# A hybrid transformer block on one core: softmax scaling and value evictions on ScalarE, the mLSTM's norm vector on transposed columns, one value product deferred

## The reference, cut to what matters

```python
# mLSTM branch
hm = mlstm_chunkwise(...)                                    # [B, S, 4, 256]
hm = hm * lax.rsqrt(jnp.mean(hm * hm, axis=-1, keepdims=True) + EPS)
hm = hm.reshape(B, S, M_WIDTH) * m_norm[i]
hm = jax.nn.sigmoid(m_o) * hm * jax.nn.silu(m_z)
# each of the three attentions
probs = jax.nn.softmax(logits, axis=-1);  out = probs @ v
# both branches
h = h + jnp.concatenate([hm, ha], axis=-1) @ w_out[i]
```

## Time and profile before

| | us |
|---|---|
| median of 3 runs (lowest, highest) | 889.74 (888.91, 890.21) |
| the profiled execution | 890.28 |
| its span from the first to the last instruction | 888.5 |
| PE busy / DVE / ACT / POOL | 854.0 / 667.8 / 451.8 / 68.4 |
| mean granted TensorE clock | 0.997 |

### The profile page before, as it was taken

How to read it: one execution, slowest core, us unless ns; L and a number is a source line. 1 busy time by engine, 2 the same in 40 slices (tenths; PEclk the granted TensorE clock), 3 DMA queues, 4 the chain that set the end, 5 groups by cost and what they waited for, 6 DMA issues and landing times.

```text
span 888.5 us, 14462 instructions
## 1 busy us (share of the span) xinstructions
PE 854.0 (96%) x5744; PEld 750.2 (84%) x5744; DVE 667.8 (75%) x1089; ACT 451.8 (51%) x719; POOL 68.4 (8%) x63
## 2 busy tenths in 40 slices
PE   8999989999999999999999999899999899999996
PEld 8989978767876898699999999579987899999995
DVE  5698798868977997789767848796777876556557
ACT  5464555454556555275454445265663654444450
POOL 1100001000001120011100100110000111001011
PEclk9999999999999999999999999999999999999998
DMA  8856677556965870899866896278617776656601
GB/s 325 305 167 193 193 237 240 180 167 201 339 236 208 276 266 1 339 328 385 278 215 224 291 354 229 94 277 332 223 45 298 287 299 202 204 163 190 191 1 47
DMA packets 56915, 200.65 MB, mean 226 GB/s; under 512 B 6600, under 2 KB 7936, under 8 KB 56848
## 3 DMA queue, kind: packets, MB, share of 16 engines
q1 hardware_dynamic: 55808, 196.50, 63.5%
q0 software_dynamic: 1040, 3.24, 1.1%
HBM read 198.57 MB, written 1.08 MB: 225 GB/s over the span
## 4 chain that ended last, share of the span: by engine, by line
PE 81%; DVE 11%; ACT 4%; issue 2%; DMA 1%; POOL 0%; DVEq 0%; SPq 0%
PE ps L1166 26%; PE ps L1167 25%; PE ps L1168 25%; DVE R L1467 2%; DVE wsp L1404 1%; PE ps L1179 1%; ACT pb L2107 1%; DVE wk L1442 1%; DMA X<-in_x 1%; PE ps L1333 1%; PE ps L1372 1%; PE ps L1258 1%; DVE small L1845 0%; PE ps L1341 0%; PE ps L1348 0%
## 5 line engine op out<-in xcount | busy, mean ns | idle before, releaser
L1166 PE MATMUL ps<-XT,wsp 128*128 128x256 f32 x760 | 215.2, 283 | 5.9 <-DVE XT L1449 3.0
L1167 PE MATMUL ps<-XT,wsp 128*128 128x256 f32 x760 | 212.5, 280 | 0.0
L1168 PE MATMUL ps<-XT,wsp 128*128 128x256 f32 x760 | 212.1, 279 | 0.0
L1404 DVE TENSOR_TENSOR wsp<-ring,wsp 128x1024 fp32r<-128x1024 f32 x141 | 175.2, 1251 | 9.1 <-ACT wsp L1949 9.0
L1949 ACT CAST wsp<-ring 128x1024 fp32r<-128x1024 f32 x140 | 145.5, 1045 | 60.7 <-PE ps L1168 53.8
L1166 PEld LDWEIGHTS ps<-XT,wsp 128*128 128x128 f32 x760 | 142.7, 188 | 10.6 <-DVE wsp L1404 4.1
L1167 PEld LDWEIGHTS ps<-XT,wsp 128*128 128x128 f32 x760 | 142.7, 188 | 0.9
L1168 PEld LDWEIGHTS ps<-XT,wsp 128*128 128x128 f32 x760 | 142.3, 187 | 0.0
L1166 PE MATMUL ps<-wsp,ra 128*128 128x512 f32 x236 | 94.5, 400 | 4.0 <-issue 1.5
L1168 PE MATMUL ps<-wsp,ra 128*128 128x512 f32 x236 | 93.6, 397 | 0.0
L1167 PE MATMUL ps<-wsp,ra 128*128 128x512 f32 x236 | 93.1, 394 | 0.0
(11 more groups left out here) (272 smaller groups left out, 1516.3 us busy)
## 6 DMA issues: line engine op xcount, KB each, us to landing
arena<-in_mod_w SPq DMA_DIRECT2D x48, 512.0 KB, 6.0
ring<-in_mod_w SPq DMA_DIRECT2D x44, 512.0 KB, 4.7
ring<-in_ffn_a SPq DMA_DIRECT2D x28, 512.0 KB, 5.0
ring<-in_ffn_b SPq DMA_DIRECT2D x28, 512.0 KB, 5.7
arena<-in_ffn_o SPq DMA_DIRECT2D x22, 512.0 KB, 4.8
ring<-in_ffn_o SPq DMA_DIRECT2D x22, 512.0 KB, 4.9
arena<-in_ffn_a SPq DMA_DIRECT2D x16, 512.0 KB, 5.1
arena<-in_ffn_b SPq DMA_DIRECT2D x16, 512.0 KB, 4.9
```

The lines of the kernel that those rows point to most:

```text
L1166: pe.matmul(o, l[0], r[0], start=start, stop=False)
L1167: pe.matmul(o, l[0], r[1], start=False, stop=False)
L1168: return pe.matmul(o, l[1], r[0], start=False, stop=stop)
L1404: ve.tensor_tensor(w[:, 1024:1024 + n], raw[slot[0]][:, 0:n], w[:, 0:n].bitcast(f32), SUB).then_inc(*done("V", "lo", u, also=[("raw", *slo ...
```

## The change

- `ev_mv` and `ev_av` are all done by ScalarE.
- The value products of the mLSTM's last head stand in the second yield of h == 4 and not in the first.
- `m_norm` lies among the constant columns. The multiplication by it in `ev_mz` and the two row loads are gone; the transposed columns of tags hm0 and hm1 are split by `xt_s` with `m_norm` as its scale, where `xt_hl` had no scale. `xt_s` now writes at the offset `k0`.
- `norm`: VectorE keeps the reciprocal; the scaling of the row is a ScalarE activation (Copy with a scale per partition). The place in the list of steps is the same.

```diff
@@ order()
-        add("ev_mv", t, cb, b, either())
+        add("ev_mv", t, cb, b, "A")
...
-                if h and j == 0:
+                if h and j == (h == 4):
...
-    proj_a("u", 8, "w_av", 0, 1, lambda t, cb, b: add("ev_av", t, b, either()))
+    proj_a("u", 8, "w_av", 0, 1, lambda t, cb, b: add("ev_av", t, b, "A"))
...
-        if t == 0:
-            rows_mn[c] = load(("row", "m_norm", c * 512), 512)
         s = wk.get()
-        add("ev_mz", t, c, b, s, prior("wk", s), rows_mn[c])
+        add("ev_mz", t, c, b, s, prior("wk", s))
         wk.put(s[0])
-        if t == 1:
-            free_raw(rows_mn[c])
...
-            transposed("hm0", 4, None)
+            transposed("hm0", 4, "s")
...
-            transposed("hm1", 4, None)
+            transposed("hm1", 4, "s")
@@ column()
+            if tag[0:2] == "hm":
+                return K("m_norm", 4 * int(tag[2]) + k), None, None
@@ vector()
-                        ve.scalar_tensor_tensor(d[1][k + i], ps[b[0]][:, i * 256:(i + 1) * 256], scale,
-                                                d[0][k + i].bitcast(f32), MUL, SUB).then_inc(
+                        ve.scalar_tensor_tensor(d[1][k0 + k + i], ps[b[0]][:, i * 256:(i + 1) * 256], scale,
+                                                d[0][k0 + k + i].bitcast(f32), MUL, SUB).then_inc(
...
                     ve.reciprocal(smx[:, i:i + 1], smx[:, i:i + 1]).then_inc(*done("V", "norm", task, i, 0))
-                    for e in new("V", ("norm", task, i, 0)):
-                        ve.wait_ge(*e)
-                    ve.tensor_scalar(p, p, smx[:, i:i + 1], None, MUL).then_inc(*done("V", "norm", task, i, 1))
...
-                    for e in new("V", ("mz", t, c, 1), ("ld", *mn)):
-                        ve.wait_ge(*e)
-                    ve.tensor_tensor(g, g, raw[mn[0]][:, 0:512], MUL).then_inc(
-                        *done("V", "mz", t, c, 2, also=[("raw", *mn)] if t else []))
@@ scalar()
-                        ac.activation(d[0][k + i], ps[b[0]][:, i * 256:(i + 1) * 256], ACT.Copy, scale=scale).then_inc(
+                        ac.activation(d[0][k0 + k + i], ps[b[0]][:, i * 256:(i + 1) * 256], ACT.Copy, scale=scale).then_inc(
...
+                elif kind == "norm":
+                    task, i, s = a
+                    p = pb[s[0]][:, 0:128 * (of(task, i)[1] + 1)]
+                    for e in new("A", ("norm", task, i, 0)):
+                        ac.wait_ge(*e)
+                    ac.activation(p, p, ACT.Copy, scale=smx[:, i:i + 1]).then_inc(*done("A", "norm", task, i, 1))
@@ layout()
-    o["m_norm"], o["norm_final"] = a["m_norm"], a["norm_final"].reshape(1, -1)
+    put("m_norm", col(a["m_norm"].reshape(-1)))
+    o["norm_final"] = a["norm_final"].reshape(1, -1)
```

More of the change, by code:

```diff
@@ L7 @@
 COLS = [("norm_in", 8), ("conv_w", 32), ("fconv_w", 132), ("fconv_b", 44), ("q_norm", 2), ("kv_norm", 2),
-        ("mod_b", 96), ("c", 8), ("b_gate", 2), ("inv_freq", 1), ("sign", 1), ("nf", 8), ("ln", 64)]
+        ("mod_b", 96), ("c", 8), ("b_gate", 2), ("inv_freq", 1), ("sign", 1), ("nf", 8), ("ln", 64),
+        ("m_norm", 8)]
 CONSTS = [("ident", 128), ("ones", 256), ("cm", 256), ("cmT", 256)]
@@ L640, in order @@
     dsa = W.beside(dsa_steps(), DSA_PACE)
-    rows_mn = {}
     def ev_moz(t, cb, b):
@@ L1672, in vector @@
                     task, i, s = a
-                    p = pb[s[0]][:, 0:128 * (of(task, i)[1] + 1)]
                     for e in new("V", ("exp", task, i)):
@@ L1701, in vector @@
                 elif kind == "ev_mz":
-                    t, c, b, s, _, mn = a
+                    t, c, b, s, _ = a
                     g = GT[:, t, c * 512:(c + 1) * 512]
@@ L1720, in vector @@
                             o = hm[:, t * 4 + h, :]
-                            for e in new("V", ("ml_rs",), ("mz", t, c, 2)):
+                            for e in new("V", ("ml_rs",), ("mz", t, c, 1)):
                                 ve.wait_ge(*e)
@@ L2132, in scalar @@
                 elif kind == "ev_mz":
-                    t, c, b, s, before, _ = a
+                    t, c, b, s, before = a
                     for e in new("A", ("fill", *b), before):
```

## The result

| | before | after |
|---|---|---|
| median (lowest, highest), us | 889.74 (888.91, 890.21) | 898.29 (897.26, 898.70) |
| the profiled execution, us | 890.28 | 898.7 |
| its span, us | 888.5 | 896.9 |
| mean granted TensorE clock | 0.997 | 0.992 |

The ratio is 1.0092 with a 95% interval of 1.0081 to 1.0103: the change makes the kernel 8.55 us slower. Slower was the forecast, but by 3.6 us, and the time lies above the range given.

The account below looks back on a forecast made before the run. TensorE, busy 854.0 of 888.5 us, was taken as the bound. Terms -0.8 - 0.2 + 3.4 + 1.2 = +3.6 us took the profiled 890.28 to 893.9, as median 893.3 us; range 888.4 to 896.5.

Parts of the forecast that it names:

- Evictions and the deferred product: mLSTM, 119 to 131 us: TensorE's wait moves from the value product to the weights' low halves; 0 us.
- The norm vector: Waits near 184 us and the next group: fewer VectorE multiplies against a longer split; -0.8 and -0.2 us.
- The second attention: Burst, 326 to 350 us: multiplies lengthen ScalarE and VectorE's alternation; maximum 3.2 us later, TensorE +3.4 us.
- what decides is the order: Softmax rows: the multiply stands behind an unrelated exp, ahead of the transposed rows' copy and the output's high half.
- The third attention's tail: 655 to 667 us: two turns with multiplies delay an output by 0.7 and the last multiply by 1.4; +1.2 us.
- its ends: The lowest and highest cost given for the third attention's tail: 0 and +1.8 us.
- the first one: Whole kernel: with the clock at 0.997 throughout, only changes to TensorE's idle time count; no size given.
- rings: Second attention's burst and third's tail: ScalarE and VectorE take turns, each multiply lengthens a turn; +4.6 us together.
- gates: The two waits around the mLSTM's gates and split, reached earlier without the norm vector's multiplies; -1.0 us together.
- faster: Rival, chance 0.18: banks and row buffers let TensorE run ahead, VectorE's relief alone counts; -2.9, 886.9 us.
- no change: Rival, chance 0.20: TensorE's slack in projection units takes most; tail costs 0.6 + 0.5 against 1.0 gained; 889.8 us.
- Slower still: Rival inside the forecast's 0.62: the multiply occupies ScalarE for its full 0.50 and 0.39 us; 894.8 us.

Follow-up runs that it names:

- evictions_and_deferral: The kernel before with only the value evictions on ScalarE and the last head's value products one unit later: 889.62 us, ratio 0.9991.
- all_but_rows_aligned: The changed kernel with VectorE scaling the softmax's rows again and 12 more unused constant columns: 887.59 us, 0.9967 of the kernel before.
- rows_only: The kernel before with only the scaling of the softmax's rows moved to ScalarE: 895.85 us, ratio 1.0064.
- change_aligned: The changed kernel with 12 unused columns behind the norm vector in the constant table: 893.68 us, 1.0039 of the kernel before.
- rows_behind_copy: The kernel before with all rows scaled on ScalarE, the multiply moved behind the copy of the transposed rows: 895.73 us, ratio 1.0055.
- aligned_again: A second measurement of the changed kernel with VectorE scaling the rows and 12 more unused constant columns: 886.98 us, 0.9961 of the kernel before.
- aligned_and_fitted: The changed kernel with VectorE scaling rows, 12 more unused columns and 9 unread multiplications in the layer norm's wait: 887.52 us, 0.9969 of before.

## Why the prediction was off

- **Evictions and the deferred product, 0:** right. `evictions_and_deferral` is equal to before within its interval, and the path is as forecast: the six small instructions stand before the next low half, TensorE is at the same matmul at 128.8 us.
- **The norm vector, -0.8 and -0.2:** the mechanism was right, the first size too large for the whole change. From 175 to 185 us the changed kernel gains 0.47, `all_but_rows_aligned` 0.77: the 0.3 between them is the rows on ScalarE, which alone cost 0.29 in that stretch of `rows_only` (`change_aligned` gains 0.49 there, with the rows on ScalarE). The prediction counted one multiply ahead of the split and also took the relief of VectorE. From 185 to 215 us the gain is 0.2 to 0.3. Measured -0.68 for -1.0.
- **The second attention, +3.4:** right in size, +3.80 from 326 to 350 us, heads of 4.27 us where 4.2 or more was forecast. Of its reason ("what decides is the order") half holds: the multiply lengthens the turn because it stands in it, but not because it stands ahead of the copy, as `rows_behind_copy` shows. In `rows_only` the maximum of 347.75 comes 3.20 us later, which is the sum's 3.2. By single steps its last four turns are as forecast, +0.67, +0.51, +0.68 and +0.48; the two ahead of them are -0.39 and +1.50 for 1.23 forecast together, and that they come out near it is luck. TensorE's idle time from 334 to 354 us is 2.7 us, not above 3, and only 1.28 of it ends with the multiply; the other waits end with an output's low half (L1689). The multiply's price, 0.50 and 0.39 us, was near: 510 and 385 ns.

```profile
L2104 ACT ACTIVATE pb<-pb,small x48: 385/443/510, 145.3 to 671.9; 128x128 f32<-128x128 f32 x24, 128x256 f32<-128x256 f32 x24
```

- **The third attention's tail, +1.2:** right as to the waits, +1.48, +1.48 and +1.43 in the three kernels with all rows on ScalarE and no fall behind the tail, within its ends.
- **The failed step** is the first one: "the granted clock is 0.997 throughout: only what adds to or takes from TensorE's idle time counts". It read the clock of before as a property of the kernel, and priced idle time by its own length. In the profiled execution TensorE was idle for 2.75 of the 24 us of the burst, where it had been for 1.03, and across the burst's end for 1.28 us in one piece, up to 350.80; from 352.81 on it ran at 1.2 GHz for 3.4 us: +1.50 behind the burst, +1.5 behind the tail, and +0.82 behind an old wait (the table's differences). In the profiled executions that is 3.9 of the 8.4 us. Of the medians less is due to it, since the kernel before has such falls in other executions (its clock lay between 0.993 and 0.999 in the repeated runs, that of the change between 0.992 and 0.996): filling two waits gave back 1.9 us. That the new waits bring the falls is argued from their place and from the filled kernel, not shown: of the four kernels with all rows on ScalarE and nothing in the waits, only the changed one has them in its trace behind the burst and the tail. The Trainium skill, page "TensorE: Matmul & The Clock Gate", section "A second HAM failure mode: psum-queue depth-cycling", describes a kernel whose matrix engine idles briefly and often between groups of matmuls and loses clock between the bursts. The waits of the burst here (0.99, 0.59, 0.60 and 1.28 us) are for ScalarE and VectorE, not of that kernel's kind. The trace agrees in so far as a fall follows them in the changed kernel; in `rows_only`, with waits of 0.93, 0.59, 0.59 and 1.26 us, none follows. The prediction should have had such a fall as a rival.
- **The missing term** is the table of constants. "`m_norm` lies among the constant columns" stands in the description of the change and in no sum. It cost 1.7 us by medians, as much as the whole "no difference" bound. With this term and the others as the traces measure them (rings +5.25 for +4.6, gates -0.68 for -1.0) the forecast of 893.3 becomes 896.0 us, still inside the range. The 2.3 us that are left are of the size of the clock's part as far as it is known (1.9 given back by the filling).

The sum with the terms as measured, on the profiled executions: -0.68 (gates), +3.80 and +1.45 (rings), +3.9 (clock), +1.2 (drifts of the layout, the differences of the table that are left), -1.23 (the beginning, which scatters) = +8.4. By medians: 6.1 to 7.6 for the rows with their falls, 1.7 for the layout, -0.4 to -1.1 for the rest, 6.7 to 8.9 together, for 8.55 measured. The 7.6 is itself a difference from the changed kernel and tests nothing; with the rows at 5.9 to 6.1 the sum is 6.5 to 7.4, and 1.2 to 2.0 us stay without a term of their own.

Of the rivals, *faster* and *no change* are out: the ring is the limit, and no slack of the projections took it up. *Slower still* came nearest in time (894.8), but named the wrong reason, a full 0.50 and 0.39 us of occupation; the activations behind the multiply start 0.40 and 0.29 us after it, as priced.

What stays open: whether the new waits make falls likelier, why a wait is followed by a fall in one execution and not in another, and which of the tiles' start addresses sets the distance of the matmuls.

## What to carry to other kernels

Moving work to the engine with more idle time helps only if it isn't in a ring with the busy one: find the turns (who waits for whom within one head), and add the moved instruction's occupation to each turn (at two places in the list the cost was the same here). Beside each new wait of the matrix engine of a microsecond or more, carry a possible fall of its clock as a term with a chance (1.5 us in one of four kernels here). Work that nobody reads in such a wait lowered the median of one kernel here and not of another, so it has to be measured. Before crediting an edit with a microsecond in 900, run the kernel before with the same change of tile addresses; a table of constants that grows is an edit of its own, and its width can be chosen.

## What was not expected of the hardware

- Unused bytes ahead of the tiles change how fast back-to-back matmuls follow each other: 119.1, 121.2 or 119.7 ns at 128x256, 233.7, 229.7 or 228.2 ns at 128x512, -2.0 to +1.7 us in the whole kernel.
- A stretch of 3.4 us at half clock can follow waits no longer than 1.28 us; `rows_only` and `change_aligned` had the same wait, 1.26 and 1.28 us long, and no fall. Executions differ in where the falls lie: with the same program up to 560 us, `aligned_again` has one at 377 us and `aligned_and_fitted` one at 183 us, 1.6 us each.
- A kernel with multiplications that nobody reads in two of its waits was faster: 1.9 us here, although they made the transposes 1.2 us late.
